# GpSimd scales the second token tile at the start, TensorE turns it inside the first unit, and three products of zeros go

## The reference, cut to what matters

```python
def rmsnorm(x, g):
    xf = x.astype(jnp.float32)
    xf = xf * lax.rsqrt(jnp.mean(xf * xf, axis=-1, keepdims=True) + EPS)
    return xf.astype(x.dtype) * g

# layer 0, first step
proj = rmsnorm(x, mix_norm_g[0]) @ w_in[0]
```

## Time and profile before

| | us |
|---|---|
| median of 3 runs (lowest, highest) | 1334.89 (1334.65, 1335.25) |
| the profiled execution, time | 1334.52 |
| the profiled execution, span | 1332.7 |
| PE busy of the span | 1310.0 |
| DVE busy | 407.1 |
| ACT busy | 333.3 |
| POOL busy | 14.8 |

### The profile page before, as it was taken

How to read it: one execution, slowest core, us unless ns; L and a number is a source line. 1 busy time by engine, 2 the same in 40 slices (tenths; PEclk the granted TensorE clock), 3 DMA queues, 4 the chain that set the end, 5 groups by cost and what they waited for, 6 DMA issues and landing times.

```text
span 1332.7 us, 24929 instructions
## 1 busy us (share of the span) xinstructions
PE 1310.0 (98%) x10817; PEld 857.7 (64%) x10817; DVE 407.1 (31%) x778; ACT 333.3 (25%) x629; POOL 14.8 (1%) x28
## 2 busy tenths in 40 slices
PE   9999999999999999998999999999999999999987
PEld 6989888888798986432667666335666335666322
DVE  6686754444748765000111100101100101100201
ACT  6565554443646642000001000001000001000002
POOL 1100000000000000000000000000000000000000
PEclk9999999999999999999999999999999999999999
DMA  8935255554543689999999999999999999999995
GB/s 322 336 130 225 95 188 186 187 187 187 185 178 120 250 341 368 405 423 421 420 420 420 420 408 396 413 420 420 420 420 419 420 421 420 419 421 419 421 421 241
DMA packets 63913, 444.27 MB, mean 333 GB/s; under 512 B 7293, under 2 KB 8717, under 8 KB 10936
## 3 DMA queue, kind: packets, MB, share of 16 engines
q1 hardware_dynamic: 61976, 437.22, 81.4%
q0 software_dynamic: 1824, 5.42, 1.1%
HBM read 441.17 MB, written 1.44 MB: 332 GB/s over the span
## 4 chain that ended last, share of the span: by engine, by line
PE 91%; DMA 4%; SPq 2%; DVE 2%; ACT 1%; issue 1%; DVEq 0%; ACTq 0%
PE up_banks L2252 34%; PE bank L2252 16%; PE bank L1752 7%; PE bank L1754 7%; PE bank L1753 7%; DMA raw<-in_moe_units 4%; PE up_banks L1752 3%; PE up_banks L1754 3%; PE up_banks L1753 3%; SPq L536 2%; PE bank L2316 1%; PE bank L2199 1%; PE bank L1847 1%; PE bank L2229 1%; PE bank L1794 1%; DVE w_lo L1053 1%
## 5 line engine op out<-in xcount | busy, mean ns | idle before, releaser
L1644 DVE TENSOR_TENSOR hidden<-hidden,up_banks 128x384 f32<-128x384 f32 (+1 forms) x56 | 27.3, 487 | 582.7 <-ACT hidden L987 582.7
L1053 DVE TENSOR_TENSOR w_lo<-raw,w_hi 128x1024 fp32r<-128x1024 f32 x154 | 181.5, 1219 | 42.0 <-ACT w_hi L660 40.7
L660 ACT ACTIVATE w_hi<-raw 128x1024 fp32r<-128x1024 f32 x154 | 155.2, 1057 | 47.6 <-PE bank L1754 39.6
L987 ACT ACTIVATE hidden<-up_banks 128x384 f32<-128x384 f32 (+1 forms) x56 | 24.5, 437 | 475.3 <-PE up_banks L2252 475.3
L2252 PE MATMUL up_banks<-raw,mid_x 128*32 128x256 f32 (+1 forms) x1260 | 95.0, 450 | 0.0
L2252 PE MATMUL bank<-raw,hT 128*32 128x256 f32 (+2 forms) x716 | 82.1, 486 | 2.7 <-DMA raw<-in_moe_units 2.6
L1752 PE MATMUL bank<-xT_hi,w_hi 128*128 128x256 f32 x288 | 82.5, 287 | 0.0
L1753 PE MATMUL bank<-xT_lo,w_hi 128*128 128x256 f32 x288 | 81.5, 283 | 0.0
L1754 PE MATMUL bank<-xT_hi,w_lo 128*128 128x256 f32 x288 | 81.4, 283 | 0.0
L2252 PEld LDWEIGHTS up_banks<-raw,mid_x 128*32 128x32 f32 x1260 | 57.4, 110 | 33.3 <-issue 1.6
L978 ACT ACTIVATE hT<-bank 128x384 f32<-128x384 f32 (+1 forms) x56 | 24.5, 437 | 209.2 <-PE bank L2316 209.2
(11 more groups left out here) (421 smaller groups left out, 2099.7 us busy)
## 6 DMA issues: line engine op xcount, KB each, us to landing
raw<-in_moe_units SPq DMA_DIRECT2D x109, 1024.0 KB, 23.0
slot_w_hi<-in_moe_units SPq DMA_DIRECT2D x46, 1024.0 KB, 23.8
slot_w_lo<-in_moe_units SPq DMA_DIRECT2D x46, 1024.0 KB, 24.2
raw<-in_layer_units SPq DMA_DIRECT2D x44, 1024.0 KB, 4.9
raw<-in_dense_units SPq DMA_DIRECT2D x33, 1024.0 KB, 4.8
slot_bias<-in_moe_units SPq DMA_DIRECT2D x19, 1024.0 KB, 22.7
slot_xT_lo<-in_moe_units SPq DMA_DIRECT2D x18, 1024.0 KB, 22.9
slot_xT_hi<-in_moe_units SPq DMA_DIRECT2D x18, 1024.0 KB, 22.8
```

Source lines behind the costliest of these rows:

```text
L660: act.activation(w_hi[:, st.split(u), half, :], raw[:, st.slot(u), half * n:(half + 1) * n], ACT.Copy)\
L987: act.activation(hidden_of(n), ups_of(n, 1), ACT.Silu).then_inc(sem("silu"), 1)
L1053: dve.tensor_tensor(w_lo[:, st.split(u), half, :], raw[:, st.slot(u), half * n:(half + 1) * n], w_hi[:, st.split(u), half, :].bitcast(F32) ...
L1644: dve.tensor_tensor(hidden_of(n), hidden_of(n), ups_of(n, 0), ALU.mult)\
```

## The change

Four things are changed. The gain of layer 0 comes from the host as an array of 128 equal rows (`first_gain`) and is loaded as it stands, where before one row was read 128 times. The scaling of tile 1 goes from DVE (two instructions) to POOL (four: per half one with `rstd`, one with the gain); DVE tells POOL through the semaphore `first_rstd`. PE turns tile 1 no longer before the first unit, but between the first and the second half of unit 0. And PE makes four products of zeros at the start instead of six, and two before the first unit instead of three.

```diff
@@ sync
-        sp.dma_start(g_row[:, :], io["mix_norm_g"][0].rearrange("(o d) -> o d", o=1).broadcast_to([P, D]))\
-            .then_inc(sem("first_gain_in"), 16)
+        sp.dma_start(g_row[:, :], io["first_gain"]).then_inc(sem("first_gain_in"), 16)
@@ gpsimd
         pool.dma_start(table, io["bias_table"]).then_inc(sem("table_in"), 16)
+        pool.wait_ge(sem("first_gain_in"), 16)
+        pool.wait_ge(sem("x_in1"), 16)
+        pool.wait_ge(sem("first_rstd"), 1)
+        for half in range(2):
+            s = slice(half * 512, (half + 1) * 512)
+            pool.tensor_scalar(xn[:, 1, s], x[:, 1, s], rstd[:, 1:2], None, ALU.mult).then_inc(sem("times_rstd"), 1)
+            pool.wait_ge(sem("times_rstd"), half + 1)
+            pool.tensor_tensor(xn[:, 1, s], xn[:, 1, s], g_row[:, s], ALU.mult).then_inc(sem("xn_ready"), 1)
         pool.wait_ge(sem(f"raw{layer_stream(0).slot(1)}"), layer_stream(0).landed(1))
@@ vector
-        root(0, 1)
-        scaled(0, 1, x_tiles)
+        root(0, 1, told="first_rstd")
@@ tensor, tile_by_tile
-            tokens_out(st, u, 4, 512, lower, banks, True, False, tiles=(0,), count=False)
+            tokens_out(st, u, 4, 512, lower, banks, True, False, which=(0,), tiles=(0,), count=False)
+            if m == 0:
+                turn_tile(0, 1, norm_banks[2:4])
+            tokens_out(st, u, 4, 512, lower, banks, True, False, which=(1,), tiles=(0,), count=False)
@@ tensor
-        zeros(6)
+        zeros(4)
         pe.wait_ge(sem("ident_in"), 16)
         turn_tile(0, 0, (0, 1))
         pe.wait_ge(sem("table_in"), 32)
         pe.matmul(bank[7][0:HEADS, 0:SKEW_W], rel[:, :], table, start=True, stop=True).then_inc(sem("skew_mm"), 1)
-        zeros(1)
-        turn_tile(0, 1, (2, 3))
         zeros(2)
@@ kernel
+    given["first_gain"] = np.tile(given["mix_norm_g"][0], (P, 1))
```

## The result

| us | before | changed |
|---|---|---|
| median (lowest, highest) of 20 runs each | 1334.69 (1332.90, 1336.28) | 1338.73 (1335.65, 1341.12) |
| profiled execution, time (span) | 1334.52 (1332.7) | 1340.72 (1338.9) |

The ratio is 1.0032, 95% interval 1.0026 to 1.0038: the change makes the kernel slower by 4.0 us, 0.3%. 1334.0 was forecast. The measured median is 0.5 above the high end of the range, 1338.2. The forecast called everything under 0.2% "the same"; with 20 runs each the interval is about 0.8 us to either side, and the loss of 4.0 is clear of it.

A forecast was written before the change was run, and what follows sets the result against it. PE, busy 98% of the span, was taken as the bound. An earlier start (-1.8) plus the moved turning (+0.87) gave -0.93: 1333.6 for the profiled execution, 1334.0 for the median, range 1332.8 to 1338.2.

The forecast's parts named there:

- What bounds the kernel: Whole kernel: PE is busy 98% of the span, and its gain or loss at the start carries to at least 330 us.
- Fewer zeros, earlier start: PE's start: with fewer products of zeros, unit 0 starts at 13.6 instead of 15.40, a gain of 1.8 us.
- The moved turning: Inside unit 0: tile 1's turning is no longer hidden in place of zeros and costs 0.87 us.
- GpSimd's four instructions: Scaling of tile 1: 1.0 us each, half 0 at 12.3 and half 1 at 14.3, so PE does not wait.
- The estimate that the prediction gives by the Trainium skill: GpSimd's scaling: 2.6 cycles an element with two inputs, about line rate with one; 3.1 to 3.8 us for all four.
- The rival of the shared port: DVE's `w_lo` beside GpSimd's last two instructions: one holds the other off, PE waits 1.2, time 1334 to 1336; chance 0.20.
- TensorE's clock: Rival at PE's start: idle gaps of 0.5 and 1.0 us slow unit 0's passes, net +2, time 1337; chance 0.07.
- The reload of GpSimd's library: Rival before GpSimd's first scaling: a late reload makes PE 4.2 late, net +3.3, time 1338.2; chance 0.13.
- Behind GpSimd's queue: Memory tokens issued after GpSimd's scaling: a delay of 2 us is covered by 5 us.
- The gain load: Early transfers: 128 rows might land gain and unit 0 0.8 earlier, net gain 1.7; nothing was taken for it.
- unit 0 landed before 11: Sign in the profile after: the broadcast load of the gain was the brake, so the forecast is wrong in size.

The follow-up runs named there:

- e6: Changed kernel without GpSimd's work: DVE scales tile 1 between the first and second `w_lo` piece; 1333.51 against 1334.95 for the kernel before, ratio 0.9992.
- e1: Changed kernel with tile 1 scaled by DVE as before instead of GpSimd; 1335.21 against 1335.03 for the kernel before, ratio 1.0000.
- e9: e6 with PE waiting for weight unit 3 between the two half turnings of tile 1; 1338.62 against 1334.81 for the kernel before, ratio 1.0026.
- e10: e9 with three products of zeros ahead of PE's wait; 1337.22 against 1334.81 for the kernel before, ratio 1.0016.
- e8: Kernel before with only the gain of layer 0 loaded as 128 rows; 1334.97 against 1334.95, ratio 1.0002.
- e5: Changed kernel, unaltered, in a second set of runs; 1339.44 against 1334.95 for the kernel before, ratio 1.0038.
- e2: Changed kernel with four more products of zeros between the two half turnings of tile 1; 1338.56 against 1335.03 for the kernel before, ratio 1.0024.
- e7: Changed kernel with DVE scaling half 0 of tile 1 and GpSimd only half 1; 1333.93 against 1334.95 for the kernel before, ratio 0.9995.
- e3: Changed kernel with DVE waiting for all of tile 1 before its first `w_lo`; 1340.76 in one run against 1335.03 for the kernel before.

## Why the prediction was wrong, by its own steps

- **What bounds the kernel.** Right. PE's start is carried whole: marks at 31 and 506 agree in thirteen profiles.
- **Fewer zeros, earlier start.** Right: 1.8 was forecast, 1.96 came; PE's first turning was at 9.11 (forecast 9.0), unit 0 at 13.44 (13.6). Unit 0's load took 8.2 instead of 8.6 and landed at 10.9, which is more than the difference.
- **The moved turning.** 0.87 was forecast. e6, without the wait, shows 0.87 and 0.13 more on the pass behind it.
- **GpSimd's four instructions: the step that failed.** "I take 1.0 each: half 0 at 12.3, half 1 at 14.3, no wait." PE waited 3.92. The step has two faults. The first is the durations: measured alone they are 1.57 and 1.27, so 5.7 in all where 4.0 was taken and 5.6 was the bound. By itself this would have made PE wait about 0.9 (10.49 + 5.8 = 16.3, asked for at 15.4), and the forecast would have been "no change". The second and larger one is that the sum put the meeting with `w_lo` at nothing and left it to a rival: it made the four 3.0 longer. The estimate that the prediction gives by the Trainium skill has the scaling by `rstd` as the cheaper instruction, and on the chip it is the dearer one.
- **The rival of the shared port, priced too low.** The mechanism was named, with the place, and given 0.20; its price was a wait of 1.2 and a time of 1334 to 1336. What came was 3.9. I let one instruction be held off, and let each of them take 1.0. In fact two were held off, one of them for 2.0, and the delay came on top of 1.7 us of longer instructions. Added up, 16.3 + 0.95 + 2.0 = 19.3, where the trace has 19.29; the 0.95 and the 2.0 are measured, and the prediction's reasoning would not have given the second.
- **TensorE's clock, priced as a rival of its own.** I hung it on gaps of 0.5 and 1.0 us, and such gaps did nothing (e1 waited 0.8 and 1.2 there, 0 slow passes), and not on the rival's wait, where it belongs. In the first profile the fall cost 2.45. By the granted clocks on record it came in at least 16 of 25 executions of the changed kernel. In the median it is worth 1.4 by e9 against e10, and 0.35 by the split of the changed kernel's own runs.
- **The reload of GpSimd's library.** The largest unknown in the forecast, and nothing: GpSimd waited for `rstd` until 10.27 and scaled from 10.49. Neither this trace nor any other here has a row in which it is seen. The forecast's range reached 1338.2 because of it, and the measured 1338.73 is near that end by luck.
- **Behind GpSimd's queue.** The memory tokens were issued at 19.2 instead of 14.1. That cost nothing: unit 2's first pass starts 4.8 before the mark in both kernels (26.16 and 30.94; 31.83 and 36.62).
- **The gain load.** Taken as nothing; in the changed kernel's first profile it took 6.5, as before. Unit 0 landed at 10.9, so the sign "unit 0 landed before 11" came without its cause being shown. What the rows give is open, as said at e8.

Against the forecast the mark is 6.6 too high: 3.92 for the wait, 2.45 for the clock, 0.39 for a turning that is cut in two (0.60 and 0.66 in e5, instead of 0.87), less 0.16 for the earlier start.

What stays open is what the clock is worth in the changed kernel's median: the filled wait of e10 is 1.4 below the unfilled one, while e2 and the split of the runs show less than 1. Each of these differences is about as large as its scatter.

## What to carry to other kernels

Before giving an idle engine a part of the chain's start, compare when it ends and when it is asked for, with durations of that engine; an engine whose trace has no such row needs one run that measures it. And ask what its instructions meet: here GpSimd and a DVE that read two operands from SBUF held each other off, which cost nothing where both ended before they were asked for (e7), and 3 us where they didn't. Price what a wait brings with it in the same line as the wait: a start that carries whole through 500 us carries its losses too, and waits of 3.0 to 7.0 us took TensorE's clock along in most executions here.

## What the runs showed of the hardware that was not expected

GpSimd multiplies 128x512 float32 by a value for each partition in 1.57 us and by another tile in 1.27; the instruction with one large operand is the slower of the two. The Trainium skill (GPSIMD Engine Reference, § 4.1) calls an operation with one input roughly line-rate, which at its 1.2 GHz would be an estimate of 0.43; the measurement decides. The 1.27 is near § 3.1, whose 2.6 cycles an element make an estimate of 1.11 before dispatch.

The rise of the clock at the start differs too: in e8 the twelve passes of zeros took 8.42 instead of 8.09, and the whole kernel was 0.31 later at the mark by that alone. After a wait of 3.0 TensorE ran at 1.2 GHz for a turning of half a tile and 7 passes, after 3.9 for as much and 10 passes, after 7.0 for 11 and a part. In e3, after a wait of 4.7, it ran so for six passes (the first is 0.77 in the chain), a whole turning (1.71 instead of 0.87) and a pass and a part more. After waits of 1.3 and 1.7 (e5) no pass was slow.
